# Dilated attention by residues: two heads a unit, one key block a tile in groups 2 and 3, group softmaxes mixed afterwards

## The reference, cut to what matters

```python
DIL_GROUPS = ((128, 1), (512, 4), (2048, 16))      # window, step
for g, (w, d) in enumerate(DIL_GROUPS):            # inside block(n), 128 queries
    offs = d * jnp.arange(w // d + 1)
    pos = t[:, None] - offs[None, :]
    sc = einsum('bhqd,bhqjd->bhqj', q_blk, kg) + bias[None, :, None, :]
    sc = where(pos >= 0, sc, -inf)
    lse = logsumexp(sc)                            # one a query, head and group
    outs.append(einsum('bhqj,bhqjd->bhqd', exp(sc - lse), vg)); lses.append(lse)
wgt = softmax(stack(lses, 0), axis=0)
o = sum(stack(outs, 0) * wgt[..., None], axis=0)   # (512, 4 heads * 64)
```

## Time and profile before

| | |
|---|---|
| median of 3 runs | 1255.31 us (1255.18 to 1255.52) |
| the profiled execution's own time | 1255.13 us |
| its span in the profile | 1253.0 us |
| TensorE busy | 1221.0 us, 97% of the span |
| mean granted clock of TensorE | 0.988 |

### The profile page before, as it was taken

How to read it: one execution, slowest core, us unless ns; L and a number is a source line. 1 busy time by engine, 2 the same in 40 slices (tenths; PEclk the granted TensorE clock), 3 DMA queues, 4 the chain that set the end, 5 groups by cost and what they waited for, 6 DMA issues and landing times.

```text
span 1253.0 us, 16295 instructions
## 1 busy us (share of the span) xinstructions
PE 1221.0 (97%) x5298; PEld 768.7 (61%) x5298; DVE 589.1 (47%) x1232; ACT 430.2 (34%) x773; POOL 302.0 (24%) x293
## 2 busy tenths in 40 slices
PE   8999999999999999999999999999999999999994
PEld 5888878877776475555555555555555555555552
DVE  6543565555553634544444444444444444444441
ACT  5333433444435212023333333333333333333332
POOL 0230011000000001133334443333343433333321
PEclk7999999999999999999999999999999999999998
DMA  6242221142312075379999999999999999999941
GB/s 206 90 162 85 68 68 35 34 135 67 102 68 101 20 301 220 128 287 335 336 332 333 336 340 335 332 342 331 339 333 340 341 333 341 336 336 333 336 146 25
DMA packets 65421, 284.10 MB, mean 227 GB/s; under 512 B 12720, under 2 KB 14256, under 8 KB 40421
## 3 DMA queue, kind: packets, MB, share of 16 engines
q1 hardware_dynamic: 51044, 249.97, 54.5%
q0 software_dynamic: 14336, 33.59, 11.4%
HBM read 270.88 MB, written 29.41 MB: 240 GB/s over the span
## 4 chain that ended last, share of the span: by engine, by line
PE 93%; DVE 2%; DMA 1%; ACT 1%; issue 1%; SPq 0%; POOL 0%; ACTq 0%; DVEq 0%
PE bank L1483 38%; PE bank L1328 21%; PE bank L1495 15%; PE bank L1509 4%; PE bank L1280 3%; PE bank L1469 2%; PE bank L1351 2%; PE bank L1370 2%; PE bank L1465 1%; PE bank L1488 1%; PE bank L1394 1%; PE bank L1381 1%; PE bank L1502 1%; DMA arena<-in_w_out 1%; DMA arena<-in_x 1%
## 5 line engine op out<-in xcount | busy, mean ns | idle before, releaser
L1483 PE MATMUL bank<-arena 128*96 128x512 f32 (+1 forms) x576 | 255.0, 596 | 0.0
L528 POOL TENSOR_TENSOR turn<-minus_half 16x1 f32<-16x1 f32 x128 | 126.7, 990 | 458.9 <-DMA out<-arena,idxs 379.1
L1483 PE MATMUL bank<-arena_x,arena 128*96 128x512 f32 x512 | 226.7, 596 | 0.0
L1495 PE MATMUL bank<-w_lo 128*96 128x512 f32 (+1 forms) x816 | 204.0, 398 | 3.9 <-issue 2.9
L1483 PEld LDWEIGHTS bank<-arena 128*96 128x96 f32 (+1 forms) x576 | 93.0, 167 | 132.6 <-issue 132.5
L1495 PEld LDWEIGHTS bank<-w_lo 128*96 128x96 f32 (+1 forms) x816 | 129.9, 166 | 51.1 <-issue 4.1
L1483 PEld LDWEIGHTS bank<-arena_x,arena 128*96 128x96 f32 x512 | 81.2, 164 | 119.1 <-issue 119.1
L1119 DVE SCALAR_TENSOR_TENSOR arena_x<-arena_x,gate,bank 96x256 f32<-96x256 f32 x64 | 30.5, 477 | 225.8 <-ACT arena_x L767 181.1
L767 ACT ACTIVATE arena_x<-bank 96x256 f32<-96x256 f32 (+1 forms) x68 | 25.8, 380 | 317.2 <-PE bank L1483 317.2
L774 ACT ACTIVATE arena<-bank 96x512 f32<-96x512 f32 x128 | 75.9, 593 | 168.1 <-PE bank L1495 166.2
L1328 PE MATMUL bank<-w_hi,hT_hi 128*128 128x512 f32 (+1 forms) x320 | 126.2, 394 | 3.0 <-DVE arena L1091 1.5
(11 more groups left out here) (156 smaller groups left out, 1552.7 us busy)
## 6 DMA issues: line engine op xcount, KB each, us to landing
arena<-in_w_gate_e SPq DMA_DIRECT2D x32, 1024.0 KB, 10.8
arena<-in_w_up_e SPq DMA_DIRECT2D x32, 1024.0 KB, 13.2
arena<-in_w_down_e SPq DMA_DIRECT2D x32, 1024.0 KB, 11.3
arena_x<-in_w_gate_e SPq DMA_DIRECT2D x32, 1024.0 KB, 10.9
arena_x<-in_w_up_e SPq DMA_DIRECT2D x32, 1024.0 KB, 13.3
arena_x<-in_w_down_e SPq DMA_DIRECT2D x32, 1024.0 KB, 11.0
arena<-in_w_in SPq DMA_DIRECT2D x14, 1024.0 KB, 5.4
arena<-in_w_gate SPq DMA_DIRECT2D x8, 1024.0 KB, 5.7
```

The costliest lines, as they stand in the source:

```text
L528: nc.gpsimd.tensor_tensor(turn[:], minus_half[0:16, 0:1], minus_half[0:16, 0:1], ALU.add).then_inc(turns, 1)
L1483: last = nc.tensor.matmul(psG[n][0:rows, :].rearrange("s (g c) -> s g c", g=2), lhs[:, j, 0:rows], wgu[slot][:, :, j, :], start=(j == 0), ...
L1495: last = nc.tensor.matmul(psY[h][0:rows, :], midT[n][a][:, j, 0:rows], w[b][:, j, h * 512:(h + 1) * 512], start=(j == 0 and k == 0), stop= ...
```

## The change

The dilated stage has 8 units u = 4w + i, each with the two heads 2w and 2w+1 of every group. For groups 2 and 3, q, k and v are stored in the order of residues modulo 4, so that a tile i holds the 128 tokens of residue i and all keys that they see; a unit has 4 score blocks a head (3 where i = 0). q and k get this order in `copy_qk`; v gets it by weight tiles of every fourth column in the dense units of chunk 3 (its second half only, so these four units are computed in two halves of 256 columns, 48 matmuls for 24) and of chunk 4. Each group has its own maximum and sum. The unnormalised results are kept transposed (`yT_a`); during the forgetting stage six statistics are transposed (TensorE, 4 transposes each, v = 1 to 5), the mixing shares are computed on 4 partitions in `share_step` (VectorE, one exponential on ScalarE), stored to DRAM, loaded back broadcast to 128 partitions, and applied at v = 8 and 9. Dense units 20 to 31 run whole, one or two in a unit. In the forgetting stage VectorE scales the weights before it makes the low parts. The transposes at its end go, w_proj_a is loaded after v = 9, and the load of x tile 3 moves behind the projection, ahead of the second w_out chunk.

Cut to its core, with four columns of indent taken off:

```diff
-UA, UB = HG * NT, HB * 2
...
+UA, UB = HG // 2 * NT, HB // 2 * NT
+def tile_a(u):
+    return u % NT
...
+    return [(0, tile_a(u) - 1)][:tile_a(u)] + [(g, tile_a(u)) for g in range(NG)]
+def first_col_a(u):
+    return P * (NG + 1 - len(blocks_a(u)))
...
+def dense_beside(u):
+    k = B_UNITS - A_UNITS
+    return range(A_UNITS + k * (u - 1) // UA, A_UNITS + k * u // UA)
...
-    bias_near = at(52, HG * 2 * P).rearrange("p (h u) -> p h u", h=HG)
-    bias_far = at(56, (HA - HG) * N).rearrange("p (h u) -> p h u", h=HA - HG)
+    bias_a = at(52, HG * (NG + 1) * P).rearrange("p (h u) -> p h u", h=HG)
...
         sp.wait_ge(vec_free, 2 * NG)
+        sp.wait_ge(vec_masked, 1)
         for g in range(NG):
-            sp.dma_start(vec_dram.ap()[g * HG:(g + 1) * HG], vec[:, g * DIST:(g + 1) * DIST]).then_inc(vec_stored, 16)
+            width = 2 * P if g else DIST
+            sp.dma_start(vec_dram.ap()[g * HG:(g + 1) * HG, 0:width], vec[:, g * DIST:g * DIST + width]).then_inc(vec_stored, 16)
         load_chunk(3)
         sp.wait_ge(vec_stored, 16 * NG)
-        for head in range(HA):
-            w = 2 * P if head < HG else N
-            toeplitz = bass.AP(vec_dram, head * DIST + N - w, [[1, P], [1, w]])
-            sp.dma_start(bias_near[:, head, :] if head < HG else bias_far[:, head - HG, :], toeplitz).then_inc(bias_in, 16)
+        for g in range(NG):
+            c0, c1, d0 = ((0, 2 * P, N - 2 * P), (2 * P, 3 * P, 0), (3 * P, 4 * P, 0))[g]
+            sp.dma_start(bias_a[:, :, c0:c1], bass.AP(vec_dram, g * HG * DIST + d0, [[1, P], [DIST, HG], [1, c1 - c0]])).then_inc(bias_in, 16)
         for c in range(4, NIN - 1):
...
             load_chunk(c)
-        sp.wait_ge(pv_psum, UA)
+        load_half(NCHUNK - 1, 0)
+        sp.wait_ge(share_ready, 1)
+        sp.dma_start(share_dram.ap(), share).then_inc(share_stored, 16)
+        sp.wait_ge(share_stored, 16)
+        for w in range(2):
+            for h in range(2):
+                src = bass.AP(share_dram, (2 * w + h) * NG * N, [[0, HEAD_DIM], [N, NG], [1, N]])
+                sp.dma_start(share_b[h * HEAD_DIM:(h + 1) * HEAD_DIM, w], src).then_inc(share_in[w], 16)
+        load_half(NCHUNK - 1, 1)
+        sp.wait_ge(combined, 2)
...
         load_chunk(NCHUNK)
         sp.wait_ge(pv_psum, UA + UB)
-        sp.wait_ge(yTa_turned[0], yTa_turned[1])
-        for t in (2, 3):
+        for t in (2,):
             sp.dma_start(x1[t], x_rows[t * P:(t + 1) * P, :]).then_inc(x1_in[t], 16)
         sp.wait_ge(proj_psum, ND)
-        for t in (0, 1):
+        for t in (0, 1, 3):
             sp.dma_start(x1[t], x_rows[t * P:(t + 1) * P, :]).then_inc(x1_in[t], 16)
...
+                    if g:
+                        m = P // NT
+                        part = part.rearrange("p h (m r) -> p h r m", r=NT)
+                        m0 = t * m if key else P - (t + 1) * m
+                        dst = dst.rearrange("p h (r m) -> p h r m", r=NT)[:, :, :, m0:m0 + m]
+                        part = part if key else part[:, :, :, ::-1]
+                    else:
+                        dst = dst[:, :, cols]
+                        part = part if key else part[:, :, ::-1]
+                    last = nc.scalar.activation(dst, part, ACT.Copy, scale=gains[:, key:key + 1])
             else:
...
                 act.wait_ge(small_in, 16 * 3)
+                if m >= 10:
+                    act.wait_ge(combined, 1 if m < 13 else 2)
...
         def exp_a(u):
             act.wait_ge(scores_ready, u + 1)
-            w = P * len(blocks_a(u))
-            nc.scalar.activation(sc_a[u % 2][:, 0:w], sc_a[u % 2][:, 0:w], ACT.Exp, bias=negmax[:, u % 2, 0:1],
-                                 accum_out=rowsum[:, u % 2, 0:1]).then_inc(exp_ready, 1)
+            i, c0 = tile_a(u), first_col_a(u)
+            for s in range(2):
+                h = 2 * (u // NT) + s
+                for g, (a, z) in enumerate(((c0, 2 * P), (2 * P, 3 * P), (3 * P, 4 * P))):
+                    last = nc.scalar.activation(sc_a[u % 2][:, s, a:z], sc_a[u % 2][:, s, a:z], ACT.Exp, bias=negmax_a[:, g, i, h:h + 1],
+                                                accum_out=rowsum_a[:, g, i, h:h + 1])
+            last.then_inc(exp_ready, 1)
...
+            if v == 1:
+                turned_stat(1, share[:, 1, :])
+            if v == 3:
+                act.wait_ge(apart_ready, 1)
+                nc.scalar.activation(share, share, ACT.Exp, scale=-1.0).then_inc(apart_exp, 1)
...
+            c0 = first_col_a(u)
             dve.wait_ge(scores_psum, u + 1)
             if u >= 2:
...
-            for g, (b0, b1) in enumerate(key_blocks_a(u)):
-                w = P * (b1 - b0)
-                u0 = P * (b0 - i) + N - P
-                row = bias_far[:, (g - 1) * HG + h, :] if g else bias_near[:, h, :]
-                u0 -= 0 if g else N - 2 * P
-                last = nc.vector.tensor_tensor(sc_a[u % 2][:, c0:c0 + w], psS[g][:, 0:w], row[:, u0:u0 + w], ALU.add)
-                c0 += w
+            for s in range(2):
+                last = nc.vector.tensor_tensor(sc_a[u % 2][:, s, c0:4 * P], psS[s][:, c0:4 * P], bias_a[:, 2 * (u // NT) + s, c0:4 * P], ALU.add)
             last.then_inc(scores_added, 1)
...
+            i, w, c0 = tile_a(u), u // NT, first_col_a(u)
+            most = rowmax_a[:, u % 2]
+            link(nc.vector.reduce_max(most[:, :, c0 // P:], sc_a[u % 2][:, :, c0:4 * P].rearrange("p s (b k) -> p s b k", k=P), AX.X))
+            if c0 == 0:
+                link(nc.vector.tensor_tensor(most[:, :, 1:2], most[:, :, 0:1], most[:, :, 1:2], ALU.max))
+            nc.vector.tensor_scalar(negmax_a[:, :, i, 2 * w:2 * w + 2].rearrange("p g s -> p s g"), most[:, :, 1:], -1.0, None,
+                                    ALU.mult).then_inc(scores_ready, 1)
+        def rows_a(u):
+            dve.wait_ge(pv_psum, u + 1)
+            i, w = tile_a(u), u // NT
+            v = psV[:, 0:NG * P].rearrange("p (g q) -> p g q", g=NG)
+            nc.vector.tensor_copy(yT_a[:, w, 0, i * P:(i + 1) * P], v[:, 0, ::-1])
+            nc.vector.tensor_copy(yT_a[:, w, 1:, i::NT], v[:, 1:, ::-1]).then_inc(y_norm, 1)
...
+            if v == 3:
+                nc.vector.tensor_tensor(share, share, least.unsqueeze(1).broadcast_to([HG, NG, N]), ALU.subtract).then_inc(apart_ready, 1)
+            if v == 4:
+                dve.wait_ge(apart_exp, 1)
+                for k, dst in ((3, total), (4, part)):
+                    (e, l), used = turned_stat(k)
+                    dst, _ = in_token_order(k % NG, dst, dst)
+                    nc.vector.tensor_tensor(dst, e, l, ALU.mult).then_inc(used, 1)
+                    dve.wait_ge(used, order[("st", k)][1] + 1)
+                link(nc.vector.tensor_tensor(total, total, part, ALU.add))
...
+            if v == 6:
+                nc.vector.tensor_tensor(share, share, total.unsqueeze(1).broadcast_to([HG, NG, N]), ALU.mult).then_inc(share_ready, 1)
+            if v in (8, 9):
+                w = v - 8
+                dve.wait_ge(share_in[w], 32)
+                link(nc.vector.tensor_tensor(yT_a[:, w], yT_a[:, w], share_b[:, w], ALU.mult))
+                link(nc.vector.tensor_tensor(yT_a[:, w, 0, :], yT_a[:, w, 0, :], yT_a[:, w, 1, :], ALU.add))
+                nc.vector.tensor_tensor(yTa[w], yT_a[:, w, 0, :], yT_a[:, w, 2, :], ALU.add).then_inc(combined, 1)
...
+            for n in dense_beside(u):
+                mean_squares(n)
+                if n != dense_beside(u)[-1]:
+                    over_norm(n)
...
+            rows_a(u - 1)
...
-            dense(B_UNITS + v - 1)
             if v < UB:
                 scale_b(v)
+            dense(B_UNITS + v - 1)
+            share_step(v)
...
+        def stationary_of(h, j, t, g):
+            return h[:, j, t::NT] if g else h[:, j, t * P:(t + 1) * P]
...
-            if j == 0:
+            halved = c == VA_LAST - 1
...
             w = [split_of(x, c, j) for x in (w_hi, w_lo)]
-            h = [x[:, j, :] for x in (hT_hi, hT_lo)]
+            g = 2 if c == VA_LAST else part
+            cols = slice(part * COLS // 2, (part + 1) * COLS // 2) if halved else slice(0, chunk_cols(c))
             for k, (a, b) in enumerate(((0, 0), (0, 1), (1, 0))):
                 if B_UNITS <= n < G_UNITS:
-                    left, right = w[a][:, t * P:(t + 1) * P], h[b]
+                    left, right = w[a][:, t * P:(t + 1) * P], (hT_hi, hT_lo)[b][:, j, :]
                 else:
-                    left, right = h[a][:, t * P:(t + 1) * P], w[b]
-                last = nc.tensor.matmul(psD[n % 2][:, 0:chunk_cols(c)], left, right, start=(j == 0 and k == 0), stop=(j == ND - 1 and k == 2))
+                    left, right = stationary_of((hT_hi, hT_lo)[a], j, t, g), w[b][:, cols]
+                last = nc.tensor.matmul(psD[n % 2][:, cols], left, right, start=(j == 0 and k == 0), stop=(j == ND - 1 and k == 2))
+            if halved and part == 0:
+                return
             if t == NT - 1 and j == HALF - 1:
```

(35 more changed lines are left out.)

170 lines of the change are left out of this document (82 added, 88 removed).

## The result

The changed kernel takes 1247.24 us (median of 4 runs, 1246.44 to 1251.50), the kernel before 1255.41 beside it: a ratio of 0.9945, 95% interval 0.993 to 0.996. That is faster by 8.2 us where 38.7 were forecast, and outside the range of 1211 to 1238. The sign was right; the size was a fifth.

What follows compares the result with a forecast made beforehand. TensorE, with work in 97% of the span, was taken as the bound, so time between matmul starts counts. -41.2 + 0.6 + 2.0 - 1.5 + 1.6 = -38.5 from 1255.1 gave 1216.6 us; range 1211 to 1238.

Steps and rivals of the forecast that it cites:

- v projection: Chunk 3 as 192 matmuls of 256 columns: +0.6 us (0.4 to 1.1), nothing for strided weight loads.
- Rival 2: v projection: strided weight loads no longer covered by the matmul, 0.104 us a step more, +20, 1237 us; chance 0.14.
- The halves: Chunk 3 of v in 256-column matmuls instead of 512: +0.6 us (0.4 to 1.1).
- Rival 3: v projection: strided split-operand loads serialise with their matmuls, 0.42 us a step, 1275 us, slower than before; chance 0.02.
- Dilated stage: Unit 1's scores to forgetting unit 1: 93.8 us of TensorE work plus 1.0 of waits, for 136.0: -41.2.
- rival 4: Dilated stage: pairing of two heads fails for 128-wide blocks, scores and sums run one after another, +16, 1233; chance 0.03.
- 1.9 us [of slack]: Dilated stage: VectorE and ScalarE need 8.1 us a unit, transposes want it at 10.0, so the chain is covered.
- Rival 1: Dilated stage: VectorE and ScalarE become the chain if adds, copies and exponentials cost 3 us more: +8, 1225; chance 0.11.
- The unit I named: Dilated stage, unit 3: forget-gate sums delay normalisation for unit 4's second dense unit; 1.0 us (0 to 4) for all such places.
- Forgetting stage with its end: Forgetting stage together +2.0 us, and its final eight transposes and copy removed, -1.5 us.
- The scaling's wait: Forgetting stage: VectorE scales weights before low parts, so TensorE's three waits for the scaling go: -1.5 us.
- x tile 3: Its load ahead of the second w_out chunk, 0.52 MB, lengthens TensorE's wait there: +1.6 us (0 to 2.1).

Runs made afterwards that it cites:

- experiment 1: Changed kernel with packed instead of every-fourth-column weight tiles in the dense units of v (wrong tokens, same instructions): 1230.23 us, ratio to before 0.982.
- Experiment 7: Kernel of experiment 6 with weighted sums ahead of the normalised transposes in units with two dense units: 1219.28 us, ratio to before 0.972.
- experiment 8: Kernel of experiment 5 with one exponential for a head's three groups, sums of groups 2 and 3 left out: 3620.72 us; only the stage counts, 95.7 us.
- experiment 6: Kernel of experiment 5 with q and k units squared and summed before weights are split: 1219.12 us, ratio to before 0.972.
- experiment 5: Changed kernel with strided v loads beside 512 columns, three work orders altered, x tile 3 between the second w_out chunk's halves: 1223.65 us, ratio to before 0.975.

## Why the prediction was wrong

**v projection: +0.6 forecast, +22.8 measured. This is the step that failed.** It said "the split operand already loads at the slower pace, and I take nothing for the stride". The inference was from equality of two durations, 192 ns for a strided load in a transpose and 192 for a packed split load, to equality of their cause. The packed split load has a length of its own, and the stride comes as well: 329 ns. The prediction also knew that the load hides only under 0.120 us of matmul, and put at nothing a load that needed 0.233. Rival 2 is what happened; it was priced at +20 (0.104 us a step) and measured at 21.8, by the steps (0.113) and by experiment 1 from the first 256-column matmul on. It had a chance of 0.14, while a rule and an extrapolation of one row spoke for it, and one coincidence of two numbers against. Its price came close partly by luck: it doubled the 52 ns that a stride adds to a load in the transposes, and there the stride hardly slows the step (0.12 for 0.11). The halves themselves cost 1.1 us for 0.6, the upper end of the range given for them, and 21.8 + 1.1 is the 22.8 to 0.1 us. (Rival 3's time adds up to 1274, not 1275, which changes nothing.)

**Dilated stage: -41.2 forecast, -32.4 measured.** The matmul part stands. Experiment 7 without its 2.7 us of waits is 94.7 us, and experiment 8 without 1.8 is 93.9, where 93.8 was worked out; from start to start the scores of a unit with the near block take 1.08 us in the changed kernel (211.84 to 212.92) and its sixteen weighted sums 1.02 (181.51 to 182.53), for 1.06 and 1.02 forecast, so rival 4 is out. What failed is the second half of the term, "1.9 us [of slack], so the chain is covered", with 1.0 us (0 to 4) for all places. 9.8 us stood there: 7.8 of waits, 1.4 at the lower clock, the rest in small things. The sum behind the slack held (7.9 us for 8.1); the chain it priced was the wrong one. Rival 1 had the right engines and about the right price, +8, but not by its reason: it wanted the adds, copies and exponentials 3 us dearer, and they were not. Experiment 8 shows that the exponentials are a link of the chain, experiment 6 that the split ahead of the squares is another. The places differ from mine. I looked for the wait at the exponentials' transposes, where the changed kernel has none; it is at the transposes of normalised q and k, which end a chain that runs on from the exponentials through the split, the squares and GpSimd. The unit I named (the forget sums, then the second dense unit of unit 4) is the one of the 2.78 us.

So the bulk of the miss is two rivals' prices together, 1216.6 + 22.2 + 8.8 = 1247.6. That the measured median is 1247.24 is luck to a few us: the terms are read from the execution of 1251.50, and the small ones left out here are worth 3.9 us. The range held each of them alone, its upper end being one rival and a little. They are not exclusive, and the price of both at once was never worked out: 1216.6 + 20 + 8 = 1244.6, outside the range.

**Forgetting stage with its end: +0.5 forecast, +1.6 measured.** The transposes of statistics cost 3.0 for 2.6. The scaling's wait fell by 0.6 and not by 1.5; 0.9 us of it remain, at the same kind of place. The new wait of 0.9 has the size forecast by luck, at another step: at 302.37 TensorE waits for a product in `share_step` that takes 1.04 us, not for those of v = 8 and 9. The projection now starts 0.9 us behind the last weighted sums begin (386.79 to 387.69), where eight transposes and a wait stood between before: 394.20 - 391.86 = 2.34, so -1.4 for a forecast of -1.5. Together 3.0 - 0.6 + 0.9 - 1.4 = 1.9, of which 1.6 is seen.

**x tile 3: +1.6 forecast, +0.2 measured** (1.72 for 1.53 us of wait), near the lower bound of 0. The forecast laid the whole transfer on TensorE's path; it ran for the most part beside other work. The stretch from the projection to output unit 2 says the same: 54.2 us after, 53.9 before, and 53.1, 52.9 and 53.2 in experiments 5 to 7, where the tile stands between the halves.

**In all**, the terms of the profiled execution are +1.4 + 22.8 - 32.4 + 1.6 + 3.0 = -3.6 us, against -8.2 of the medians. The 4.6 us between are of the size of 1.4 at the start and 2.8 in the experts, where the change does nothing and the executions differ among themselves; their cause stays open.

## What to carry to other kernels

A strided view of a split stationary operand was free here only while its load stayed under the matmul's time, so put it beside the widest moving operand there is, and look up how many columns share 16 bytes. When two instructions take the same time, do not conclude that the cost of one is contained in the other. And when work is merged on one engine (two heads a unit), follow the chain past its last new instruction, through what was queued behind it, and price the rivals in pairs when they do not exclude each other (here the order of old work in the queues was worth 6.1 us of the stage, 103.5 to 97.4, without one instruction less).

## What was unexpected in the hardware

- The step of a 256-column matmul with split float32 operands rises with the 16-byte pieces that the weight load opens: 0.120, 0.120, 0.173, 0.233, 0.241 us for every, every second, third, fourth and eighth column. Distance alone does nearly nothing. Plain float32 transposes that load every eighth column start 0.12 us apart all the same.
- A wait of 2.8 us cost another 1.4 us through a lower granted clock (0.63 over the 4.1 us from its end), and taking 2.4 us of waits away in experiment 6 gave 4.3. Of two waits of 2.48 us in experiment 5, one was followed by a clock of 0.60, the other by 1.00.
- One program varies by some 5 us between executions (1251.50 and 1246.44 of the same kernel). Across the kernels' profiles, parts that no edit touches differ by 2.1 us (start to the first dense matmul) and 2.8 us (experts); in such a kernel a gain of 1 us has to be read in its stretch.
